# The recurrent branch of the second mixer in one stage: seven doubling levels inside 128-token tiles in place of 16-token chunks

## The chip, the cores and the metric

The kernel runs on one core of a Trainium2 chip. The metric is the device time of one execution in microseconds (us). A core has five engines that run their own instruction streams and meet at semaphores: PE (matmul; its weight loads are a row of their own, PEld, and overlap it), DVE (vector), ACT (scalar, with function tables that have to be loaded), POOL (GpSimd) and SP, which here issues the DMAs. SBUF and PSUM have 128 partitions; a tile "128x512" has 512 numbers in each.

## The reference

Two transformer blocks run one after the other over 512 tokens of width 1024. The second block's mixer has two halves: an attention group (its result is `n_otok` in the kernel, 8 heads of 64) and a gated linear recurrence. Their outputs, 512 wide each, are laid side by side and multiplied by `w_out` (1024 by 1024). The recurrence, for each of 4 heads with 128 key and 128 value features:

```
qf = silu(q);  f = lb + (1 - lb) * sigmoid(z);  logf = log(max(f, 1e-30))
kf = (1 - lb) * sigmoid(-z);  vf = i_in
for chunks of 64 tokens:
    b = cumsum(logf)                                  # inside the chunk
    decay[t, s] = exp(b[t] - b[s])  for s <= t, else 0   # one per key feature
    a[t, s] = sum_d qf[t, d] * decay[t, s, d] * kf[s, d]
    o = a @ vf + (qf * exp(b)) @ state
    state = exp(b_last) * state + (kf * exp(b_last - b)).T @ vf
o = o * rsqrt(mean(o * o) + 1e-6) * out_norm;  o = o * silu(g_in)
```

The size of the chunk is free: any tiling that gives the same sums is the same function. All of it is float32.

## The kernel before

The program is a row of stages; each is a block in which the five engines run their own lists of instructions, and ends in a meeting of all of them, after which SP clears the stage's semaphores. Nothing of the next stage, its DMAs included, is issued before that. The order of the work on each engine is the order in which the Python code writes it; there is no scheduler.

`x_hi`/`x_lo` hold a float32 tensor as two parts in a faster format. A dense product is three matmuls (`three_products`, L51 to L56): high by high, high by low, low by high. Weights are split the same way while they stream in: ACT makes the high part, POOL or DVE subtracts it from the raw panel for the low part. A matmul of plain float32 operands shows in the trace as two MATMUL records.

Four stages stand between the last attention stage (`att2`) and the second feed-forward stage (`ffn2`):

1. `turn_to_features` (L1167): the attention result is transposed by 16 PE transposes and split into `x_hi[:, :4]`, `x_lo[:, :4]`.
2. `hgrn_operands` (L2187): loads the 16 projected panels (4 MB, each of the four groups `z`, `inp`, `q`, `gate` 1 MB), and makes sigmoids, logarithms, a scan that sums the logs inside chunks of 16 tokens, and exponentials of the sums; transposes values and keys to token-major (`h_vtok`, `h_wtok`).
3. `hgrn_outputs` (L2336): works on chunks of 16 tokens. Inside a chunk, each distance `j` from 0 to 15 between query and key is a round: DVE subtracts the shifted log sums (L2531), ACT takes the exponential (L2488), POOL multiplies by the keys (L2520), DVE multiplies by the queries (L2567) and sums over features (L2570) into `ho_weights`. Beside it, 31 state steps go from chunk to chunk: PE makes the chunk's update `ho_kv` (L2427, 4 matmuls), DVE adds it to the decayed state (L2550, 4 instructions), PE reads the state with the chunk's queries (L2435, 4 matmuls of 16 columns). 27 of the steps are written between the rounds on DVE (`steps_by`, `BESIDE`), 4 behind them. Then 16 DMAs place the weights in a DRAM scratch, one DMA loads them back as full 128x128 matrices (`ho_inner`), PE multiplies them with the values (L2455), and the result is normed (a ones-matmul, four 128x512 reciprocals at L2584) and gated. The attention half of the output projection, 8 panels (`out_panel`, L54 to L56 with tile `ho_bank`), is written on PE behind all the state steps: four panels before L2455, four beside the norm.
4. `project_onto` (L763, tiles `wo_`): the recurrence's half of the output projection, 8 panels of 12 matmuls, added to `hT` by DVE (L385).

Of the kernel before, what the change touches and what calls it, by code (L numbers as in the profile page):

```python
# [13 lines left out]
P = 128  # L14
# [2119 lines left out]
def second_mixer(nc, hT, x_hi, x_lo, d):  # L2134
    with ExitStack() as ctx:
# [48 lines left out]
N_PROJ3 = 16  # L2184


def hgrn_operands(nc, projections, proj, ident, write, fold, ends, v_tok, w_tok, lower_bound):  # L2187

    with ExitStack() as ctx:
        c = Chip(nc, ctx)
        lb = c.sb("hf_lb", [P, HG_HEADS])
        lb_e = c.sb("hf_lbe", [P, HG_HEADS])
        free = c.sb("hf_free", [P, HG_HEADS])
        sig = c.sb("hf_sig", [P, HG_HEADS, SEQ])
        tiny = c.sb("hf_tiny", [P, HG_HEADS, SEQ])
        inside = c.sb("hf_inside", [P, HG_HEADS * SEQ])  # L2200
        part = c.sb("hf_part", [P, 1], I32)
        odd = c.sb("hf_odd", [P, 1], I32)
        parity = c.sb("hf_parity", [P, 2])
        banks = [c.ps(f"hf_bank{i}", [P, SEQ]) for i in range(4)]
        S = {x: c.sem(f"hf_{x}") for x in ("lb", "lb_shift", "lb_exp", "const", "sigmoids", "f", "seq", "logs",
                                           "b", "eb", "rest", "erest", "w", "turned", "taken")}
        landed = {x: c.sem(f"hf_landed{x}") for x in (HQ, HF, HI, HG)}
        q, z, inp, gate = (proj[:, x:x + 4, :] for x in (HQ, HF, HI, HG))

# [3 lines left out]
        def chunked(x):  # L2213
            return flat(x).rearrange("p (c i) -> p c i", i=CHUNK)
        HALF = [slice(0, 2), slice(2, 4)]
        PART = 2.0 ** -50
        with nc.Block() as block:
            @block.sync
            def _(sp):
                sp.dma_start(lb[:], lower_bound).then_inc(S["lb"], 16)  # L2220
                for x in (HF, HI, HQ, HG):
                    sp.dma_start(proj[:, x:x + 4, :], projections[x:x + 4].rearrange("n p s -> p n s")
                                 ).then_inc(landed[x], 16)

            @block.gpsimd
            def _(pool):
                pool.memset(inside[:], 1.0).then_inc(S["const"], 1)
                pool.iota(part[:], pattern=[[0, 1]], base=0, channel_multiplier=1).then_inc(S["const"], 1)
                pool.wait_ge(S["const"], 2)
                pool.memset(inside[:].rearrange("p (c i) -> p c i", i=CHUNK)[:, :, 0:1], 0.0  # L2230
                            ).then_inc(S["const"], 1)

            @block.scalar
            def _(act):
                act.wait_ge(S["lb_shift"], 1)
                act.activation(lb_e[:], lb_e[:], ACT.Exp).then_inc(S["lb_exp"], 1)
                act.wait_ge(landed[HF], 16)
                for e in HALF:
                    act.activation(flat(sig[:, e]), flat(z[:, e]), ACT.Sigmoid).then_inc(S["sigmoids"], 1)
                for e in HALF:  # L2240
                    act.activation(flat(write[:, e]), flat(z[:, e]), ACT.Sigmoid, scale=-1.0
                                   ).then_inc(S["sigmoids"], 1)
                act.wait_ge(landed[HQ], 16)
                act.activation(flat(q), flat(q), ACT.Silu).then_inc(S["sigmoids"], 1)
                act.wait_ge(landed[HG], 16)
                act.activation(flat(gate), flat(gate), ACT.Silu).then_inc(S["sigmoids"], 1)
                for n, e in enumerate(HALF):
                    act.wait_ge(S["f"], 2 * n + 2)
                    act.activation(flat(z[:, e]), flat(z[:, e]), ACT.Ln).then_inc(S["logs"], 1)
                    act.activation(flat(tiny[:, e]), flat(tiny[:, e]), ACT.Ln, scale=1.0 / PART  # L2250
                                   ).then_inc(S["logs"], 1)
                for n, e in enumerate(HALF):
                    act.wait_ge(S["b"], n + 1)
                    act.activation(flat(tiny[:, e]), flat(z[:, e]), ACT.Exp).then_inc(S["eb"], 1)
                    act.wait_ge(S["rest"], n + 1)
                    act.activation(flat(sig[:, e]), flat(sig[:, e]), ACT.Exp).then_inc(S["erest"], 1)

            @block.vector
            def _(dve):
                done = [0]  # L2260

                def then(instruction):
# [4 lines left out]
                dve.wait_ge(S["const"], 3)  # L2267
                then(dve.tensor_scalar(odd[:], part[:], CHUNK.bit_length() - 1, 1, ALU.logical_shift_right,
                                       ALU.bitwise_and))
                then(dve.tensor_copy(parity[:, 1:2], odd[:]))  # L2270
                then(dve.tensor_scalar(parity[:, 0:1], parity[:, 1:2], -1.0, 1.0, ALU.mult, ALU.add))

                dve.wait_ge(S["lb"], 16)
                dve.tensor_tensor(lb_e[:], lb[:], lb[:], ALU.subtract).then_inc(S["lb_shift"], 1)
# [5 lines left out]
                for n, e in enumerate(HALF):  # L2280
# [497 lines left out]
```

## Time and profile before

| | us |
|---|---|
| median of three runs | 3402.12 (3399.36 to 3403.47) |
| the profiled execution | 3402.71 |
| its span | 3401.0 |
| from the first transpose of stage 1 to the first DMA of `ffn2` | 2731.79 to 2999.65 |

| engine | busy us | share of the span | instructions |
|---|---|---|---|
| PE | 3071.7 | 90% | 14558 |
| PEld | 2598.3 | 76% | 14558 |
| DVE | 1909.9 | 56% | 3857 |
| ACT | 1061.0 | 31% | 1477 |
| POOL | 869.4 | 26% | 509 |

The shares are means over the whole program. The change touches one stretch of 268 us near its end, so that stretch is what has to be read. PEclk in the rows is the granted clock of TensorE as a share of 2.4 GHz: 1.00 is 2.4 GHz and 0.50 is 1.2 GHz.

### The profile page before, as it was taken

Reading aid. Unit: us, or ns where it says so; the run is one execution under the profiler, and the core shown is the slowest. Engines: PE = TensorE matmul, PEld = TensorE weight load, DVE = VectorE, ACT = ScalarE, POOL = GpSimd, SP = SyncE. Lnnn points to the kernel's source line nnn. Section 1 sums busy time; section 2 is a strip of 40 time slices with the busy share of each in tenths; the row PEclk is TensorE's granted clock in tenths of the full one; section 3 lists DMA queues with packets and bytes.
Section 4 is the critical chain, followed back from the end, with each engine's and each line's share of the span. In section 5 each row is a group of like instructions: output and inputs, shape, how many; then the busy total and the mean of one; then the engine's idle time right before and its main releaser. Section 6 shows DMA issues by size and latency. Waiting matters only on the chain. (4 is left out here: it accounts for less than half of the span.)

```text
span 3401.0 us, 41723 instructions
## 1 busy us (share of the span) xinstructions
PE 3071.7 (90%) x14558; PEld 2598.3 (76%) x14558; DVE 1909.9 (56%) x3857; ACT 1061.0 (31%) x1477; POOL 869.4 (26%) x509
## 2 busy tenths in 40 slices
PE   7669879999899999899999989998869958789997
PEld 6447667888688888699999978887657748668885
DVE  5565444866577770188888754434225468554433
ACT  3222331333244443233333333223113341132321
POOL 0013200444333334486666300000412123100000
PEclk9769989999999999899999999999869965799998
DMA  4013232344345555499999823332212020123331
GB/s 136 18 43 106 99 105 81 127 137 133 120 143 185 183 177 175 154 368 378 353 356 352 294 82 98 99 99 87 113 41 75 32 79 0 40 92 99 93 99 62
DMA packets 183698, 469.15 MB, mean 138 GB/s; under 512 B 23937, under 2 KB 75777, under 8 KB 181890
## 3 DMA queue, kind: packets, MB, share of 16 engines
q1 hardware_dynamic: 159874, 374.93, 33.4%
q0 software_dynamic: 22528, 67.19, 5.2%
q10 hardware_dynamic: 1152, 25.17, 1.8%
q8 instruction: 83, 1.36, 0.2%
q14 instruction: 61, 0.50, 0.0%
HBM read 396.49 MB, written 70.52 MB: 137 GB/s over the span
## 5 line engine op out<-in xcount | busy, mean ns | idle before, releaser
L54 PE MATMUL cb_y<-cb_g_hi,cb_b_hi 128*128 128x384 f32 x1024 | 343.1, 335 | 15.0 <-DVE cb_g_lo L1746 15.0
L55 PE MATMUL cb_y<-cb_g_lo,cb_b_hi 128*128 128x384 f32 x1024 | 342.9, 335 | 0.0
L56 PE MATMUL cb_y<-cb_g_hi,cb_b_lo 128*128 128x384 f32 x1024 | 342.8, 335 | 0.0
L186 DVE TENSOR_TENSOR ffn_lo<-ffn_raw,ffn_hi 128x1024 fp32r<-128x1024 f32 x132 | 161.4, 1225 | 271.1 <-ACT ffn_hi L182 271.1
L54 PE MATMUL ffn_bank<-x_hi,ffn_hi 128*128 128x512 f32 x704 | 277.5, 394 | 23.0 <-DVE x_lo L122 20.2
L55 PE MATMUL ffn_bank<-x_lo,ffn_hi 128*128 128x512 f32 x704 | 275.4, 391 | 0.0
L56 PE MATMUL ffn_bank<-x_hi,ffn_lo 128*128 128x512 f32 x704 | 275.1, 391 | 0.0
L491 POOL TENSOR_TENSOR bs_lo<-bs_raw,bs_hi 128x1024 fp32r<-128x1024 f32 x72 | 174.7, 2427 | 320.3 <-ACT bs_hi L468 320.3
L54 PE MATMUL bs_ps<-x_hi,bs_hi 128*128 128x512 f32 x576 | 232.3, 403 | 14.8 <-POOL bs_lo L491 14.8
L182 ACT CAST ffn_hi<-ffn_raw 128x1024 fp32r<-128x1024 f32 x132 | 137.9, 1048 | 298.9 <-PE ffn_bank L56 260.0
L56 PE MATMUL bs_ps<-x_hi,bs_lo 128*128 128x512 f32 x576 | 226.8, 394 | 0.0
L1722 ACT CAST cb_b_hi<-cb_b_raw 128x1024 fp32r<-128x1024 f32 x128 | 134.6, 1052 | 294.6 <-PE cb_y L56 267.1
L55 PE MATMUL bs_ps<-x_lo,bs_hi 128*128 128x512 f32 x576 | 225.1, 391 | 0.0
L54 PEld LDWEIGHTS cb_y<-cb_g_hi,cb_b_hi 128*128 128x128 f32 x1024 | 192.9, 188 | 15.4 <-DVE cb_b_lo L1743 15.4
L1806 POOL DMA_INDIRECT cb_rows<-in_peer_v,ex_chosen x128 | 186.9, 1460 | 59.8 <-issue 36.7
L1743 DVE TENSOR_TENSOR cb_b_lo<-cb_b_raw,cb_b_hi 128x1024 fp32r<-128x1024 f32 x128 | 156.6, 1224 | 79.9 <-ACT cb_b_hi L1722 79.9
L1603 DVE TENSOR_SCALAR br_col<-ex_iota,br_slot 128x128 f32<-128x128 f32 x384 | 196.0, 510 | 0.0
L491 POOL TENSOR_TENSOR rs_lo<-rs_raw,rs_hi 128x1024 fp32r<-128x1024 f32 x56 | 149.8, 2677 | 179.6 <-ACT rs_hi L468 179.6
L55 PEld LDWEIGHTS cb_y<-cb_g_lo,cb_b_hi 128*128 128x128 f32 x1024 | 192.9, 188 | 0.0
L56 PEld LDWEIGHTS cb_y<-cb_g_hi,cb_b_lo 128*128 128x128 f32 x1024 | 192.8, 188 | 0.0
L1787 POOL DMA_INDIRECT cb_units_of<-hidden,ex_chosen x128 | 152.6, 1193 | 116.9 <-DVE cb_total L1752 79.6
L54 PE MATMUL rs_ps<-x_hi,rs_hi 128*128 128x512 f32 x448 | 177.6, 396 | 0.5 <-POOL rs_lo L491 0.5
(483 smaller groups left out, 6992.0 us busy)
## 6 DMA issues: line engine op xcount, KB each, us to landing
cb_b_raw<-in_peer_v SPq DMA_DIRECT2D x128, 512.0 KB, 7.0
ffn_raw<-in_gu SPq DMA_DIRECT2D x88, 512.0 KB, 3.5
bs_raw<-in_peer_u SPq DMA_DIRECT2D x72, 512.0 KB, 3.6
rs_raw<-in_peer_u SPq DMA_DIRECT2D x56, 512.0 KB, 3.6
routing<-br_out ACTq DMA_DIRECT2D x8, 3072.0 KB, 9.1
cb_route<-routing SPq DMA_DIRECT2D x32, 768.0 KB, 9.2
cb_unit<-hidden SPq DMA_DIRECT2D x128, 192.0 KB
ffn_raw<-in_down SPq DMA_DIRECT2D x44, 512.0 KB, 3.5
```

What stands on the lines that cost most here:

```text
L54: pe.matmul(out, w_high, x_high, start=first, stop=False)
L55: pe.matmul(out, w_high, x_low, start=False, stop=False)
L56: return pe.matmul(out, w_low, x_high, start=False, stop=last)
L182: act.copy(hi[:, k % R, :], raw[:, k % R, :]).then_inc(high, 1)
L186: dve.tensor_tensor(lo[:, k % R, :], raw[:, k % R, :], hi[:, k % R, :].bitcast(F32), ALU.subtract).then_inc(split, 1)
L491: eng.tensor_tensor(self.lo[:, s, :], self.raw[:, s, :], self.hi[:, s, :].bitcast(F32), ALU.subtract).then_inc(self.split, 1)
L1603: last = dve.tensor_scalar(col_hot[:, k, b, :], iota[:], slot[:, k, 1, b:b + 1], None, ALU.is_equal)
L1722: act.copy(b_hi[:, j, :], b_raw[:, j, :]).then_inc(b_high, 1)
L1743: dve.tensor_tensor(b_lo[:, j, :], b_raw[:, j, :], b_hi[:, j, :].bitcast(F32), ALU.subtract).then_inc(b_split, 1)
L1787: pool.indirect_dma_start(units_of[:, n:n + 1], None, flat, bass.IndirectOffsetOnAxis(chosen[:, 1, n:n + 1], 0)).then_inc(units_landed[n / ...
L1806: pool.indirect_dma_start(rows[:, n % V, :], None, table, bass.IndirectOffsetOnAxis(chosen[:, 0, n:n + 1], 0)).then_inc(rows_landed[n % V] ...
```

## The change

The four stages become one, `hgrn_stage`. Inside a 128-token tile the scores are made in seven levels of doubling. At level `n` (block size 2^n) a query in the second half of a pair of blocks meets the keys in the first half: `qp` holds the query times the decay from its block's start, `kr` the key times the decay to its block's end, so their product is one matmul per head and tile, of which only the blocks next to each other are wanted. A mask, made by POOL, picks these out of PSUM into `hg_pairs` by `copy_predicated`. Then DVE doubles the blocks: late queries are multiplied by the total of the early block, early keys by the total of the late one. Logarithms, scan and exponentials fall away (the decays are products of `f`). The state goes from tile to tile in three steps in place of 31. The 16 (head, tile) pairs are cut in two halves `e` of 8, so that PE and DVE can take turns. The output projection is one loop over 16 half-width panels with a ring of four buffers; panels 0 to 7 (attention half) are written between the levels. The norm squares token-major results with an accumulating ACT instruction, so the reciprocal is 128x4 and no ones-matmul is left. `hg_scratch` and its 18 DMAs are gone.

```diff
-        hgrn(nc, hT, x_hi, x_lo, o_tok, ident, d)
-
-    project_onto(nc, "wo2", x_hi[:, 4:8, :], x_lo[:, 4:8, :], d["w_out"][:, :, 4 * P:], hT)
+        hgrn_stage(nc, d["hg_proj"], o_tok, ident, d["lower_bound"], d["out_norm"], d["w_out"], x_hi, x_lo, hT)
...
+                def load_out(k):
+                    if k >= R:
+                        sp.wait_ge(S["split"], k - R + 1)
...
+                sp.dma_start(lb[:], lower_bound).then_inc(S["lb"], 16)
+                load(HF)
+                load_out(0)
+                load_out(1)
+                load(HQ)
+                load(HI)
+                load_out(2)
+                load_out(3)
+                load(HG)
...
+                def level(n, e):
+                    if n:
+                        pe.wait_ge(S["doubled"], 2 * (n - 1) + e + 1)
+                        pe.wait_ge(S["masked"], 2 * (n - 1) + e + 1)
+                    else:
+                        pe.wait_ge(S["key"], e + 1)
+                        pe.wait_ge(S["query"], e + 1)
+                    for i in range(HT):
+                        a = e * HT + i
+                        to = s_ps[e][:, i * P // 2:(i + 1) * P // 2].rearrange("p (b i) -> p b i", i=1 << n)
+                        last = pe.matmul(to, flat(kr[:])[:, a * P:(a + 1) * P], second_half(flat(qp[:]), 1 << n, a),
+                                         start=True, stop=True)
+                    last.then_inc(S["scored"], 1)
...
+                pe.wait_ge(S["o_low"], 4)
+                out_panel(0)
+                out_panel(1)
+                level(0, 0)
+                level(0, 1)
...
+                same_token(0)
+                same_token(1)
+                for n in range(1, LEVELS):
+                    level(n, 0)
+                    level(n, 1)
+                    if n < 5:
+                        out_panel(n + 1)
+                pe.wait_ge(S["doubled"], 2 * LEVELS)
+                pe.wait_ge(S["masked"], 2 * LEVELS)
+                turn_keys(0)
+                turn_keys(1)
...
+                write(0)
+                pe.wait_ge(S["state"], 1)
+                turn_keys(2)
+                out_panel(6)
+                write(1)
+                read(1)
+                write(2)
+                out_panel(7)
+                turn_result(0)
+                read(2)
+                read(3)
+                for t in range(1, TILES):
+                    turn_result(t)
+                pe.wait_ge(S["y_low"], TILES)
+                for k in range(n_out // 2, n_out):
+                    out_panel(k)
...
+                def double(n, e):
+                    dve.wait_ge(S["scored"], 2 * n + e + 1)
...
+                    dve.tensor_tensor(late, late, both[:, :, 0:1].broadcast_to(late.shape), ALU.mult)
+                    dve.tensor_tensor(early, early, both[:, :, 1:2].broadcast_to(early.shape), ALU.mult)
+                    dve.tensor_tensor(totals[n + 1][:, e * half // 2:(e + 1) * half // 2], both[:, :, 0], both[:, :, 1],
+                                      ALU.mult).then_inc(S["doubled"], 1)
...
+                def place(n, e):
...
+                    dve.copy_predicated(to[:, :, :, 1, :], mask.broadcast_to(shape),
+                                        s_ps[e][:].rearrange("p (a b i) -> p a b i", a=HT, i=size)
+                                        ).then_inc(S["masked"], 1)
...
+                for n in range(LEVELS):
+                    for e in range(2):
+                        if n == 0:
+                            dve.wait_ge(S["paired"], e + 1)
+                        double(n, e)
+                        place(n, e)
+                    if n == 1:
+                        place_same(0)
+                        place_same(1)
+                    if 2 <= n <= 5:
+                        add_out(n)
```

DVE before, in the 16 rounds of stage 3; `ho_pair` is the work tile of a round, `ho_state` the state:

```order
L2531 TENSOR_TENSOR ho_pair<-ho_b 128x1536
L2550 SCALAR_TENSOR_TENSOR ho_state<-ho_state,h_ends,ho_kv 128x128 x8
L2567 TENSOR_TENSOR ho_pair<-ho_pair,ho_q 128x1792
L2570 TENSOR_REDUCE ho_weights<-ho_pair 128x14
L2531 TENSOR_TENSOR ho_pair<-ho_b 128x1408
L2550 SCALAR_TENSOR_TENSOR ho_state<-ho_state,h_ends,ho_kv 128x128 x12
L2567 TENSOR_TENSOR ho_pair<-ho_pair,ho_q 128x1664
```

DVE now, at level 2 and the first half of level 3; `hg_qp` and `hg_kr` are the folded queries and keys, `hg_total` the block totals, `hg_s` the PSUM tile of scores:

```order
L2486 TENSOR_TENSOR hg_qp<-hg_qp,hg_total 128x128x4
L2487 TENSOR_TENSOR hg_kr<-hg_kr,hg_total 128x128x4
L2488 TENSOR_TENSOR hg_total<-hg_total 128x128
L2501 COPY_PREDICATED hg_pairs<-hg_masks,hg_s 128x128x4
L2486 TENSOR_TENSOR hg_qp<-hg_qp,hg_total 128x128x4
L2487 TENSOR_TENSOR hg_kr<-hg_kr,hg_total 128x128x4
L2488 TENSOR_TENSOR hg_total<-hg_total 128x128
L2501 COPY_PREDICATED hg_pairs<-hg_masks,hg_s 128x128x4
L2474 TENSOR_TENSOR hT<-hT,hg_out 128x512
L2486 TENSOR_TENSOR hg_qp<-hg_qp,hg_total 128x64x8
```

A round of three instructions over up to 2048 numbers and 8 to 12 small state instructions has become a level half of four instructions over at most 512, with the addition of one output panel behind each level.

PE before, in the same place (`ho_kv` the update of the state, `ho_o` the read):

```order
L2427 MATMUL ho_kv<-h_vtok,h_wtok 128x128 x4
L2435 MATMUL ho_o<-h_fold,ho_state 128x16 x4
L2427 MATMUL ho_kv<-h_vtok,h_wtok 128x128 x4
L2435 MATMUL ho_o<-h_fold,ho_state 128x16 x4
L2427 MATMUL ho_kv<-h_vtok,h_wtok 128x128 x4
```

PE now, at levels 4 to 6 and just behind them (a panel is 12 rows of L54 to L56, the last two of panel 5 are shown; `hg_ktok` and `hg_vtok` are keys and values by token):

```order
L55 MATMUL hg_out<-x_lo,hg_hi 128x512
L56 MATMUL hg_out<-x_hi,hg_lo 128x512
L2306 MATMUL hg_s<-hg_qp,hg_kr 128x64 x32
L2322 MATMUL hg_s<-n_ident,hg_kr 128x128 x8
L2380 MATMUL hg_o<-hg_vtok,hg_pairs 128x128 x16
L2330 MATMUL hg_s<-hg_vtok,hg_ktok 128x128 x4
L2322 MATMUL hg_s<-n_ident,hg_kr 128x128 x4
L54 MATMUL hg_out<-x_hi,hg_hi 128x512
```

The dense panels, which stood behind the whole recurrence, now stand between the levels; levels 5 and 6 (the x32 row) have none beside them.

## Rows read from the trace of the kernel before

**Rows 1.** Windows: us, each engine's busy us (instructions), granted clock, DMA share, GB/s.
```profile
2737.70:2780.20 42.50, 7.35 (x32) 6.55 (x32) 30.26 (x44) 21.18 (x19) 2.21 (x3) 0.55 0.28 99
...
2790.00:2903.80 113.80, 99.78 (x425) 92.65 (x425) 97.34 (x151) 19.08 (x20) 46.57 (x18) 0.51 0.02 5
2903.80:2920.50 16.70, 16.70 (x72) 15.69 (x73) 4.49 (x16) 0.00 (x0) 0.00 (x0) 0.50 0.31 72
...
2934.50:2967.50 33.00, 19.36 (x89) 13.53 (x87) 28.03 (x25) 10.33 (x16) 3.87 (x3) 0.89 0.05 16
2967.50:2999.60 32.10, 23.54 (x96) 19.00 (x96) 10.61 (x17) 4.96 (x8) 0.00 (x0) 0.84 0.22 66
```

**Rows 2.** Timeline: start us, us, engine, line, op, tiles, count; edges of the four stages.
```profile
2731.79 3.59 PE L1180 MATMUL on_turn_bank<-n_ident,n_otok 128*128 128x128 f32 x16 [2.23 <-PEq L44]
...
2738.10 2.47 SPq L2222 DMA_DIRECT2D h_proj<-hg_proj  x4
...
2743.98 2.00 ACT L2239 ACTIVATE hf_sig<-h_proj 128x1024 f32<-128x1024 f32 x2 [1.71 <-DMA h_proj<-hg_proj]
...
2965.04 2.49 DVE L2594 TENSOR_TENSOR x_lo<-ho_q,x_hi 128x512 fp32r<-128x512 f32 x4
...
2970.39 10.19 SPq L336 DMA_DIRECT2D wo_raw<-in_w_out  x8
2999.65 0.33 SPq L77 DMA_DIRECT2D ffn_gain<-in_ffn_norm  x1
```

**Rows 3.** Groups by line, 2731 to 3000: busy us, mean ns, idle before, releaser.
```profile
L2427 PE MATMUL ho_kv<-h_vtok,h_wtok 32*128 32x128 f32 x248 | 62.1, 426 | 0.0
...
L2550 DVE SCALAR_TENSOR_TENSOR ho_state<-ho_state,h_ends,ho_kv 128x128 f32<-128x128 f32 x120 | 33.6, 342 | 23.7 <-PE ho_kv L2427 23.2
L2567 DVE TENSOR_TENSOR ho_pair<-ho_pair,ho_q 128x2048 f32<-128x2048 f32 (+15 forms) x16 | 31.4, 1960 | 1.2 <-POOL ho_pair L2520 1.2
```

**Rows 4.** Timeline of PE, plain float32 matmuls; one call is two records.
```profile
2679.86 1.00 PE L625 MATMUL att_o<-n_vsel,att_probsT 128*128 128x64 f32 x8
...
2852.41 2.07 PE L2427 MATMUL ho_kv<-h_vtok,h_wtok 32*128 32x128 f32 x8
...
2934.49 3.73 PE L2455 MATMUL ho_o<-ho_inner,h_vtok 128*128 128x128 f32 x32
```

**Rows 5.** Timeline of the 8 panels of `project_onto`: first matmul, last addition.
```profile
2974.42 0.79 PE L54 MATMUL wo_ps<-x_hi,wo_hi 128*128 128x512 f32 x1 [16.86 <-DVE wo_lo L370]
...
2998.00 0.69 DVE L385 TENSOR_TENSOR hT<-hT,wo_ps 128x512 f32<-128x512 f32 x1 [2.03 <-PE wo_ps L56]
```

**Rows 6.** Groups by line and shape: busy us, mean ns of one, idle before.
```profile
L255 DVE TENSOR_TENSOR ffn_prod<-ffn_scaled 128x512 f32<-128x512 f32 x44 | 30.5, 692 | 2.0 <-ACT ffn_scaled L224 0.7
...
L2584 DVE RECIPROCAL ho_b<-ho_q 128x512 f32<-128x512 f32 x4 | 13.4, 3341 | 0.0
...
L569 DVE TENSOR_SCALAR yb<-att_o,att_inverse 128x128 f32<-128x128 f32 x16 | 5.6, 351 | 2.6 <-PE att_o L625 2.1
...
L2291 DVE TENSOR_SCALAR n_otok<-n_otok,hf_free 128x512 f32<-128x512 f32 x4 | 1.9, 484 | 0.1
```

**Rows 7.** Same view, ACT and POOL.
```profile
L584 ACT ACTIVATION_READ_ACCUMULATOR att_probs<-att_biased,att_shift 128x1 f32 x80 | 14.9, 186 | 0.0
...
L2481 ACT CAST ho_out_hi<-ho_out_raw 128x512 fp32r<-128x512 f32 x8 | 4.9, 620 | 37.9 <-PE ho_bank L56 37.9
...
L2488 ACT ACTIVATE ho_pair<-ho_pair 128x128 f32<-128x128 f32 x1 | 0.3, 311 | 1.2 <-DVE ho_pair L2531 1.2
...
L2511 POOL TENSOR_TENSOR ho_out_lo<-ho_out_raw,ho_out_hi 128x512 fp32r<-128x512 f32 x8 | 11.6, 1449 | 51.3 <-ACT ho_out_hi L2481 51.3
```

**Rows 8.** Windows, columns as in rows 1: the granted clock in three stretches.
```profile
2640.00:2729.00 89.00, 89.00 (x467) 65.05 (x466) 37.78 (x158) 33.41 (x77) 11.61 (x5) 1.00 0.10 33
2850.00:2880.00 30.00, 28.55 (x121) 26.35 (x120) 25.74 (x45) 4.01 (x4) 9.37 (x4) 0.50 0.00 1
...
2959.00:2962.00 3.00, 0.00 (x0) 0.00 (x0) 3.00 (x3) 0.62 (x1) 0.00 (x0) 0.75 0.00 0
```

More of the change, by code:

```diff
@@ new lines, in hgrn_stage @@
+        kr = c.sb("hg_kr", [P, HG_HEADS, SEQ])
+        qp = c.sb("hg_qp", [P, HG_HEADS, SEQ])
+        totals = [f[:].rearrange("p h s -> p (h s)")] + [
+            c.sb(f"hg_total{n}", [P, HG_HEADS * SEQ >> n])[:] for n in range(1, LEVELS + 1)]
+        pairs = c.sb("hg_pairs", [P, HG_HEADS * TILES, P])
+        masks = c.sb("hg_masks", [P, LEVELS, P // 2])
+        v_tok = c.sb("hg_vtok", [P, TILES, HG_HEADS * P])
+        k_tok = c.sb("hg_ktok", [P, TILES - 1, HG_HEADS * P])
+        state = c.sb("hg_state", [P, TILES - 1, HG_HEADS, P])
@@ L2243, in _ @@
+                out_high(0)
+                out_high(1)
                 act.wait_ge(landed[HQ], 16)
-                act.activation(flat(q), flat(q), ACT.Silu).then_inc(S["sigmoids"], 1)
-                act.wait_ge(landed[HG], 16)
[L2246 to L2256, printed above, removed]
+                for e in HALF:
+                    act.activation(flat(q[:, e]), flat(q[:, e]), ACT.Silu).then_inc(S["silu"], 1)
+                for t in range(TILES):
+                    act.wait_ge(S["v_turned"], t + 1)
+                    act.copy(v_tok[:, t, :], o_ps[t][:]).then_inc(S["v_copied"], 1)
@@ new lines, in _ @@
+                out_high(2)
+                out_high(3)
+                act.wait_ge(landed[HG], 16)
+                act.activation(flat(gate), flat(gate), ACT.Silu).then_inc(S["gated"], 1)
+                for k in range(R, R + 6):
+                    out_high(k)
+                for t in range(TILES - 1):
+                    act.wait_ge(S["k_turned"], t + 1)
+                    act.copy(k_tok[:, t, :], s_ps[t % 2][:]).then_inc(S["k_copied"], 1)
+                square(0)
+                out_high(R + 6)
@@ new lines, in mean, with norm @@
+                def mean(t):
+                    dve.wait_ge(S["squared"], t + 1)
+                    dve.tensor_scalar(root[:, t], squares[:, t], 1.0 / P, EPS, ALU.mult, ALU.add).then_inc(S["mean"], 1)
+                def norm(t):
+                    dve.wait_ge(S["root"], t + 1)
+                    dve.reciprocal(inverse[:, t], root[:, t]).then_inc(S["inverse"], 1)
+                    dve.wait_ge(S["inverse"], t + 1)
+                    for h in range(HG_HEADS):
+                        cols = slice(h * P, (h + 1) * P)
+                        last = dve.tensor_scalar(y_tok[:, t, cols], o_ps[t][:, cols], inverse[:, t, h:h + 1], None, ALU.mult)
+                    last.then_inc(S["normed"], 1)
@@ new lines, in _ @@
+                norm(0)
+                add_out(6)
+                step(2)
+                add_out(7)
+                mean(1)
+                norm(1)
+                gated(0)
+                mean(2)
+                norm(2)
+                low_result(0)
+                gated(1)
+                mean(3)
+                norm(3)
+                low_result(1)
+                gated(2)
+                low_result(2)
+                gated(3)
+                low_result(3)
+                for k in range(n_out // 2, n_out):
+                    add_out(k)
@@ L2615, in final_norm @@
+    clear_semaphores(nc, [*S.values(), *landed.values(), *out_landed])
 def final_norm(nc, hT, gain, out):
```

560 lines of the change are left out of this document (230 added, 330 removed).

## The prediction, written before the changed kernel had run

> **What bounds the kernel now.** I read the shares of the engines first: PE is busy for 90% of the span, which says that time comes only from stretches in which PE does little dense work. The windows then show the stretch of the change, 2731.7 to 2999.6, and what each engine does in it [rows 1]. Its longest piece is the 113.8 us of the 16 rounds, 2790.0 to 2903.8. There DVE is busy for 97.3 us and PE for 99.8, yet PE does no dense product: its clock stands at 0.51, and its work is 128-column updates and 16-column reads. The groups by line say what DVE's 97 us are: 33.6 us are 120 state instructions of 0.342 us, and 31.4 us one of the three instructions of a round [rows 3]. State steps and rounds share DVE, so both are the bound; a step waits for PE too (23.2 us under L2550). Behind the loop come 16.7 us of last steps, while the weights go through DRAM; 33.0 us in which DVE is busy for 28.0, with four reciprocals of 3.34 us [rows 1, 6]; and 32.1 us for `project_onto`, 7 of them before its first matmul [rows 1, 2, 5]. In front, `hgrn_operands` takes 42.5 us with PE busy for 7.4. From the first transpose at 2731.8 to the first DMA of `ffn2` at 2999.7 it is 267.9 us [rows 2]. `ffn2` starts from nothing, so all that the stretch loses, the kernel loses.
>
> **The change, step by step.** I lay the new stage out from T, its first transpose. A hand-off is left out of each step and comes as one term at the end.
>
> *To panels 0 and 1: T+20.0.* The 16 transposes take 3.6 us [rows 2]. The first projection load (1 MB) lands 5.9 us after its issue (2738.1 to 2744.0), so at about T+6.1; before, it was issued only after stage 1. Then ACT has four sigmoids of 1.0 us each (2.00 for two, rows 2), so the high parts of panels 0 and 1 (0.62 each, rows 7), written behind them, end at 11.3, and POOL's low part, 1.45 as a mean [rows 7], at 12.6 with what DVE makes it slower. POOL's two memsets and 14 mask instructions have until T+10.6, more than 0.6 us each, and are hidden. PE has idled since T+3.6 and starts low: eight panels from a standstill take 24.3 us with the last addition, 2974.4 to 2998.7 [rows 5]; with 2.8 us for a panel at 2.4 GHz (12 matmuls of 0.234), the first costs some 4.6. Two panels: 7.4, to T+20.0. DVE's keys and queries are ready at T+16, beside it.
>
> *Level 0, values, same-token scores: T+33.0.* A level half is 8 matmuls of 64 columns. The nearest row is L625: four calls of that size in 1.00 us at 2.4 GHz, so 2.0 per half [rows 4]. Bounds: 1.9 by the 128-column L2455 (16 calls in 3.73, so 0.23 each), 4.1 by L2427 at 1.2 GHz (0.52 each). Both halves 4.0, to 24.0; value transposes 1.8; 16 same-token calls of 128 columns 3.7, to 29.6. DVE may not fold before the same-token scores are taken. Its half of level 0 is three multiplications and one masked copy over 512 numbers. Multiplications are 0.692 [rows 6], 0.62 start to start. `copy_predicated` is in no row; by the nearest (a two-operand 128x512) it is 0.69, below it 0.48 (L2291, one operand), above it 3.34 (L2584, the slowest of this size). I take 0.69. The second half ends at 33.0.
>
> *Levels 1 to 4: T+58.2.* PE does half, half, panel: 2.0 + 2.0 + 2.8 = 6.8. DVE does two halves of 2.2 to 2.4 and one addition of 0.69: at most 5.4 (level 1 has four masked copies more, 7.8, once). So PE is the bound, and DVE's work lies under the panel. Level 1 starts at 30.4 and waits for DVE's second half: its panel ends at 37.8. Three more periods make 58.2. Panels 2 to 5 cost nothing of their own here; before, all eight attention panels stood behind the steps.
>
> *Levels 5 and 6: T+69.4.* No panel is left, so the engines take turns: PE half 2.0, DVE half 2.2, with the other half between, plus an addition. 11.2.
>
> *Values and state: T+84.8.* Transposes 0.9, 16 matmuls of `hg_pairs` with the values 3.7, first write 0.9, DVE's copy 0.7, transposes 0.5, panel 6 2.8, write, read, write 2.8 (0.93 each, rows 4), panel 7 2.8. The chain of 31 steps, 3.8 us apart where PE sets it (2.07 for the update, the rest the read), is now three.
>
> *Norm: T+102.7.* ACT squares a tile in four pieces of 0.31 + 0.19, 2.0 us [rows 7]; DVE norms it with four of 0.351 [rows 6], about 1.3 with the small reciprocal; gate and low part 0.7 each, high part 0.62. ACT and DVE wait on each other tile by tile: behind panel 7, 3.2 us until the first tile is gated, then 5.7 for each of the next two, and 3.3 for the last gate, high and low part: 17.9. The four reciprocals (13.4 us) go.
>
> *Panels 8 to 15: T+127.0.* They wait for the last low part, PE has idled: 24.3 as in rows 5.
>
> *What I add.* 4 us for hand-offs that no neighbour hides (some 40 at 0.1; my bounds are 0 and 10), and the clearing of 50 semaphores. `hgrn_outputs` cleared 32 between 2967.5 and 2970.4, 2.9 us [rows 2]; I take 3.4.
>
> Sum: 127.0 + 4 + 3.4 = 134.4 in place of 267.9, so 133.5 saved. The profiled execution has 3402.7 (span 3401.0, 1.7 around it), which is 0.6 above the median of the runs. 3402.7 - 133.5 = **3269 us**.
>
> **Whether the clock holds.** PE was fully busy in the attention stage at 1.00, with 64-column matmuls between dense ones, and busy for 28.55 of 30 us in the rounds at 0.50 [rows 8]. So being busy did not bring the clock up. The levels look like the first of these as long as panels are between them, and I count 2.4 GHz; in levels 5 and 6 the waits are under 3 us, and the clock fell in a wait of about that length [rows 8]. The Trainium skill ("TensorE: Matmul & The Clock Gate", "Part 1: The HAM clock gate") says that the gate opens by how busy the PE has been; by it the levels would run at 2.4 GHz and the sum stands. The 28.55 of 30 us at 0.50 speak against taking it at its word, and so the next case has a chance.
>
> **The rivals.**
>
> *A: the clock stays at 1.2 GHz through the levels.* For: the rounds' 0.50. Against: the attention stage's 1.00. A half costs 4.1, a panel 5.1, a period 13.3: +26 for levels 1 to 4, +11 for level 0 with transposes and same-token scores, +10 for levels 5 and 6, +8 for values and state. 3269 + 55 = 3324. If it falls only in levels 5 and 6 and behind, +15: 3284.
>
> *B: DVE is dearer than I count,* by masked copies or by the short runs of 1 to 64 numbers that the levels read. 18 masked copies at 3.34 would be +48 on DVE. PE's slack in levels 1 to 4 (1.4 each) hides 6: 3269 + 42 = 3311. At twice 0.69, which two passes over the data would be, +12 less 6: 3275. Then DVE sets the period of the levels.
>
> *C: slower than before.* Every fold and masked copy works on patterns of short runs and repeated elements, and PE and DVE wait on each other at each of the 14 halves, so a price per run has no cover. There are 46 instructions of 512 numbers (28 folds, 14 + 4 masked copies) and two full-size totals. To eat 133.5 us plus 6 of slack they need 2.9 us more each, 3.6 in all, above the slowest row of that size, 3.34 [rows 6]. At 4.0 us each: 3269 + 48 * 3.3 - 6 = 3421.
>
> *D: the stage gives back what it gains elsewhere.* `ffn2` loads and normalizes only after it, so nothing speaks for this.
>
> **How the numbers follow.** The forecast, with DVE and PE near the nearest rows, has 0.62 and by itself 3255 to 3285: hand-offs of 0 to 10 us, a partly low clock, masked copies up to twice 0.69. A has 0.15 (3284 to 3324), B beyond double 0.18 (3275 to 3311), C 0.02, D 0.01, and 0.02 are left for a stage shorter than 3255. The range for 8 in 10 leaves out the ends of A, B and C: 3250 to 3308. About 0.2% is what a measurement of this kernel can tell from no change; A and B are both far below 3395, so faster 0.97, within 0.2% 0.01, slower 0.02.
>
> **What would show it right or wrong.** The new stage spans 134 us. The level matmuls stand 0.25 us apart under a granted clock near 1.00, periods of levels 1 to 4 are 6.8 us with PE without a wait, and `hg_qp`, `hg_kr` and `hg_pairs` rows read 0.69. Levels 5 and 6 take 11 us, the norm 18, and the last eight panels 24. A shows as 0.50 in the levels' windows; B as masked copies or folds over 1 us and PE waiting for DVE in levels 1 to 4; C as DVE rows over 3.6. I am wrong in the mechanism if the stage is 134 us but PE waits in loaded levels, or if the saving is not in the rounds and steps.

## The result and the profile after

The changed kernel takes **3269.84 us** (median of 4 runs, 3269.61 to 3272.06) beside 3401.69 for the kernel before (4 runs, 3399.36 to 3403.47): a ratio of 0.9614, 95% interval 0.9598 to 0.9631. The forecast was 3269 us. The profiled execution took 3270.03, its span is 3268.0.

The new stage starts with its first transpose at T = 2732.37, and `ffn2` issues its first DMA at 2867.44: 135.1 us, where the forecast had 134.4 and the kernel before 267.9 [rows 2]. From that DMA to the end of the span it is 400.6 us after and 401.3 before, so the saving lies in the stage. The windows show the stage piece by piece, with the columns of [rows 1].

```profile
2732.40:2744.40 12.00, 3.64 (x17) 3.27 (x17) 8.17 (x17) 9.79 (x13) 9.55 (x18) 0.50 0.84 307
2744.40:2751.90 7.50, 7.50 (x24) 6.03 (x25) 5.16 (x6) 2.16 (x3) 1.52 (x1) 0.72 0.77 279
2751.90:2761.00 9.10, 9.10 (x81) 8.84 (x79) 2.19 (x3) 4.92 (x8) 2.27 (x2) 1.00 0.01 2
2761.00:2765.30 4.30, 0.08 (x2) 0.06 (x1) 4.30 (x4) 1.00 (x2) 4.04 (x3) 1.00 0.60 170
2765.30:2776.50 11.20, 11.20 (x45) 10.21 (x46) 10.10 (x15) 0.00 (x0) 0.00 (x0) 0.54 0.10 29
2776.50:2795.50 19.00, 19.00 (x134) 17.50 (x133) 14.70 (x29) 1.86 (x3) 3.80 (x3) 1.00 0.14 42
2795.50:2806.00 10.50, 7.55 (x66) 7.31 (x65) 8.64 (x18) 0.62 (x1) 1.27 (x1) 1.00 0.07 27
2806.00:2822.60 16.60, 15.81 (x101) 14.58 (x102) 4.83 (x16) 5.95 (x22) 1.28 (x1) 0.90 0.06 17
2822.60:2838.80 16.20, 4.80 (x33) 3.73 (x31) 10.25 (x27) 5.69 (x24) 0.15 (x1) 0.74 0.00 0
2838.80:2864.10 25.30, 24.53 (x96) 19.74 (x96) 5.50 (x8) 2.49 (x4) 6.29 (x5) 0.89 0.03 10
```

What was 130.5 us of rounds and last steps before, 2790.0 to 2920.5 [rows 1], is now the 54.1 us of levels with their panels (2751.9 to 2806.0) and part of the 16.6 us behind them. The 132.8 us that the stage saves lie in three places: 38.6 ahead of the rounds (58.2 us from the first transpose to 2790.0 before, 19.6 to the first level now), 76.4 in the rounds and last steps (130.5, now 54.1), and 17.7 behind them (79.1, now 61.4). In levels 2 to 4 PE is busy for all of 19.00 us at a clock of 1.00. The timeline of the same stage (start us, us, engine, line, operation, tiles, count, the wait before it) holds the edges, and the one place that went otherwise than forecast.

```profile
2751.93 3.68 PE L2306 MATMUL hg_s<-hg_qp,hg_kr 128*128 128x64 f32 x32
2755.44 1.92 PE L2364 MATMUL hg_o<-n_ident,hg_all 128*128 128x128 f32 x16
2757.21 3.84 PE L2316 MATMUL hg_o<-hg_all,hg_kr 128*128 128x128 f32 x32
2758.73 6.31 POOL L2280 TENSOR_TENSOR hg_lo<-hg_raw,hg_hi 128x512 fp32r<-128x512 f32 x4 [12.81 <-ACT hg_hi L2408]
2759.50 1.07 DVE L2486 TENSOR_TENSOR hg_qp<-hg_qp,hg_f 128x512 f32<-128x512 f32 x1 [6.68 <-PE hg_o L2316]
2760.48 1.76 DVE L2487 TENSOR_TENSOR hg_kr<-hg_kr,hg_f 128x512 f32<-128x512 f32 x1
2762.17 1.74 DVE L2488 TENSOR_TENSOR hg_total<-hg_f 128x512 f32<-128x512 f32 x1
2763.83 1.29 DVE L2501 COPY_PREDICATED hg_pairs<-hg_masks,hg_s 128x512 f32<-128x512 uint32 x1
...
2765.27 6.68 PE L2306 MATMUL hg_s<-hg_qp,hg_kr 128*128 128x64 f32 x32 [4.22 <-DVE hg_pairs L2501]
2771.71 0.77 PE L54 MATMUL hg_out<-x_hi,hg_hi 128*128 128x512 f32 x1
...
2776.49 3.68 PE L2306 MATMUL hg_s<-hg_qp,hg_kr 128*128 128x64 f32 x32
...
2779.99 0.70 DVE L2501 COPY_PREDICATED hg_pairs<-hg_masks,hg_s 128x512 f32<-128x512 uint32 x1
...
2782.83 3.68 PE L2306 MATMUL hg_s<-hg_qp,hg_kr 128*128 128x64 f32 x32
...
2805.96 1.30 PE L2322 MATMUL hg_s<-n_ident,hg_kr 128*128 128x128 f32 x8 [2.40 <-DVE hg_pairs L2501]
...
2838.84 0.79 PE L54 MATMUL hg_out<-x_hi,hg_hi 128*128 128x512 f32 x1 [3.56 <-DVE x_lo L2551]
...
2867.44 0.33 SPq L77 DMA_DIRECT2D ffn_gain<-in_ffn_norm  x1
```

A level is one row of 32 records in 3.68 us, 1.75 per half. The next level starts 6.3 us later, and PE does not wait. Level 1 is the exception: DVE starts level 0 at 2759.50, when the same-token scores of the first half are taken; its first three multiplications take 1.07, 1.76 and 1.74 us where most later ones of that size take 0.69, the masked copy takes 1.29, and PE stands still for 4.22 us. The clock is still 1.00 in that wait and falls to 1.2 GHz as PE comes back (0.54 in the window, 6.68 us for the same 32 records, 0.77 for the first matmul of panel 2), and level 1 with its panel takes 11.2 us where the later levels take 6.3.

### The profile page after: what moved, and what is told of

Its sections match the earlier page's. It is cut to its first block and busy times, and to the rows that moved or that the text cites. A ratio compares the mean times of both kernels' runs of the same rounds, so it can differ in the third digit from the quotient of the medians.

```text
span 3268.0 us, 41012 instructions
## 1 busy us (share of the span) xinstructions
PE 2983.4 (91%) x14322; PEld 2521.2 (77%) x14322; DVE 1804.2 (55%) x3734; ACT 1029.6 (32%) x1475; POOL 844.8 (26%) x511
## 5 line engine op out<-in xcount | busy, mean ns | idle before, releaser
L54 PE MATMUL cb_y<-cb_g_hi,cb_b_hi 128*128 128x384 f32 x1024 | 343.2, 335 | 15.0 <-DVE cb_b_lo L1743 15.0
L56 PE MATMUL cb_y<-cb_g_hi,cb_b_lo 128*128 128x384 f32 x1024 | 342.8, 335 | 0.0
L54 PE MATMUL ffn_bank<-x_hi,ffn_hi 128*128 128x512 f32 x704 | 277.7, 394 | 25.2 <-DVE x_lo L122 23.1
L56 PE MATMUL ffn_bank<-x_hi,ffn_lo 128*128 128x512 f32 x704 | 275.4, 391 | 0.0
L54 PE MATMUL bs_ps<-x_hi,bs_hi 128*128 128x512 f32 x576 | 232.3, 403 | 14.8 <-POOL bs_lo L491 14.8
L56 PE MATMUL bs_ps<-x_hi,bs_lo 128*128 128x512 f32 x576 | 226.9, 394 | 0.0
L54 PEld LDWEIGHTS cb_y<-cb_g_hi,cb_b_hi 128*128 128x128 f32 x1024 | 192.9, 188 | 15.5 <-DVE cb_b_lo L1743 15.4
L56 PEld LDWEIGHTS cb_y<-cb_g_hi,cb_b_lo 128*128 128x128 f32 x1024 | 192.9, 188 | 0.0
L54 PE MATMUL rs_ps<-x_hi,rs_hi 128*128 128x512 f32 x448 | 177.6, 396 | 0.5 <-POOL rs_lo L491 0.5
```

What stands on the lines that cost most here:

```text
L54: pe.matmul(out, w_high, x_high, start=first, stop=False)
L56: return pe.matmul(out, w_low, x_high, start=False, stop=last)
```

## The experiments

The theory at this point: the stage is as forecast, and the 6 us at level 1 come from three things in a row: POOL's subtractions slow DVE down, masked copies with short runs cost twice as much, and PE's wait lets the clock fall. The rivals are given with each run. Times are medians; kernels of one group share their runs of the kernel before: 3400.41 (8 runs) for the first four, 3401.32 (9 runs) for the last four. The time from the stage's first transpose to `ffn2`'s first DMA in the profiled execution is given beside them: ahead of the stage all these kernels are the same, and yet that transpose starts between 2728.1 (run 7) and 2732.8 (run 1), so some us of a difference between two executions can lie outside the stage.

### 1 and 2. Rounds and steps of the kernel before, each alone

*Steps only* takes the 16 rounds out of the kernel before, on DVE, ACT and POOL:

```diff
-                for j in range(CHUNK):
-                    x = pair[:, j % 3, :CHUNK - j, :]
-                    if j + 2 < CHUNK:
-                        diff(j + 2)
...
-                for n in range(BESIDE, N_CHUNKS - 1):
+                for n in range(N_CHUNKS - 1):
                     step(n)
```

> The kernel before without the 16 rounds: the scores inside a chunk are left out, the 31 state steps stay. Theory (PE's chain of updates and reads at 1.2 GHz bounds the loop as much as DVE's rounds): 31 steps of about 3.8 us are 118 us, so the stretch from the first update (2790) to the last read (2920.5) shrinks by only 10 to 15 us, and the kernel reads 3385 to 3395. Rival (the rounds are the bound, the steps lie in their shade and would run in about half the time alone): the loop falls to 60 to 75 us and the kernel to 3340 to 3355.

*Rounds only* takes the 31 steps out, on PE and DVE:

```diff
-                for n in range(N_CHUNKS):
-                    if n < N_CHUNKS - 1:
...
-                            last = pe.matmul(kv_ps[n % 2][:, h, :], w_tok[rows, n % 2, tile, cols],
...
-                for n in range(BESIDE, N_CHUNKS - 1):
-                    step(n)
```

> The kernel before without the 31 state steps: the state and its part of the output are left out, the 16 rounds stay. Theory (rounds and steps share DVE): DVE's three instructions of a round are 74 us in all, with the start and the turns between engines some 80 to 85 in place of 113.8, and the 16.7 us of last steps go as far as the DMAs of the weights do not need them. Panels 0 to 3 come before the loop's end. Kernel 3402 - 30 - 25 = 3347, 3335 to 3360. Rival (POOL and ACT bound the rounds): the rounds stay near 100 us and the kernel near 3370.

Measured: steps only 3384.14 (ratio 0.9952, 0.9936 to 0.9968), rounds only 3350.06 (0.9851, 0.9832 to 0.9871). So taking the rounds away alone saves 16 us, a little more than expected, and the steps alone 50, as expected; the stretch to `ffn2` has 251.4 and 216.7 us in place of 267.9. First a window of *steps only*, then the first matmul behind the rounds in *rounds only*.

```profile
2850.00:2920.00 70.00, 70.00 (x299) 63.57 (x298) 18.47 (x60) 3.52 (x6) 5.15 (x4) 0.58 0.04 12
```

```profile
2867.45 0.77 PE L54 MATMUL ho_bank<-x_hi,ho_out_hi 128*128 128x512 f32 x1 [66.99 <-DVE hT L2518]
```

Without rounds PE is busy for 70.00 of 70.00 us, with the steps and from 2903.89 with the panels: the steps are a chain of their own on PE, and DVE is nearly free (18.47). From the first update (2790.75) to panel 0 (2903.89) the steps take 113.1 us alone, of 130.5 with the rounds. Without steps PE stands still for 66.99 us while DVE, ACT and POOL do the rounds, and the first DMA of the weights is issued at 2866.80 instead of 2903.85. The two lay beside each other, and each hid most of the other. That is why a change to these two saves more than 50 us only if it takes both away. No run takes both away and leaves the rest of the four stages as it was, and none separates what made the 38.6 us ahead of the rounds.

### 3. What a masked copy costs, and what POOL does to DVE

The changed kernel with a row of DVE instructions behind the stage, each of 128x512 numbers and each waiting for the one before; at the end the same beside POOL's subtractions. They write only buffers that are no longer read.

```diff
+                    masked(0, 0, s_ps[0][:])
+                    masked(1, 1, s_ps[0][:])
+                    masked(2, 2, s_ps[0][:])
+                    masked(6, 6, s_ps[0][:])
+                    masked(6, 0, s_ps[0][:])
+                    masked(0, 6, s_ps[0][:])
+                    masked(0, 0, from_sbuf)
+                    masked(2, 2, from_sbuf)
+                    plain(0, s_ps[0][:])
+                    plain(2, s_ps[0][:])
+                    fold(0)
```

> The changed kernel with a row of DVE instructions of 512 numbers behind its stage, first with POOL idle, then with POOL subtracting. Theory P (the pattern written): a masked copy into runs of 1 or 2 numbers takes 1.29 us, into runs of 4 or more 0.70, whatever the mask and the source; an ordinary multiplication into the same runs takes 0.69. Rival M (the mask's contents or its repeats): with the mask of level 0 in the layout of level 6 it takes 1.29 as well. Rival S (PSUM as source): from SBUF the masked copy of level 0 takes 0.70. Under POOL's subtractions (two SBUF operands) theory C (DVE and POOL share the way to SBUF) says that multiplications with two SBUF operands go from 0.69 to 1.1 to 1.8, and those with one PSUM operand stay at 0.7.

The first number is the level whose pattern is written (runs of 2 to that power), the second the mask. The kernel took 3305.89 us in its one run, 36 of it for the added row. Its timeline:

```profile
2863.93 1.29 DVE L2643 COPY_PREDICATED hg_pairs<-hg_masks,hg_s 128x512 f32<-128x512 uint32 x1 [0.32 <-PEq L2238]
2865.25 1.29 DVE L2643 COPY_PREDICATED hg_pairs<-hg_masks,hg_s 128x512 f32<-128x512 uint32 x1
2866.58 0.69 DVE L2643 COPY_PREDICATED hg_pairs<-hg_masks,hg_s 128x512 f32<-128x512 uint32 x1
...
2868.06 0.72 DVE L2643 COPY_PREDICATED hg_pairs<-hg_masks,hg_s 128x512 f32<-128x512 uint32 x1
2868.82 1.29 DVE L2643 COPY_PREDICATED hg_pairs<-hg_masks,hg_s 128x512 f32<-128x512 uint32 x1
2870.14 1.30 DVE L2643 COPY_PREDICATED hg_pairs<-hg_masks,hg_all 128x512 f32<-128x512 uint32 x1
...
2872.21 0.69 DVE L2650 TENSOR_TENSOR hg_pairs<-hg_s,hg_masks 128x512 f32<-128x512 f32 x1
...
2884.94 14.67 POOL L2626 TENSOR_TENSOR hg_lo<-hg_raw,hg_hi 128x512 fp32r<-128x512 f32 x10 [30.85 <-DVEq L2670]
2884.95 2.93 DVE L2643 COPY_PREDICATED hg_pairs<-hg_masks,hg_s 128x512 f32<-128x512 uint32 x4
2887.91 6.55 DVE L2656 TENSOR_TENSOR hg_qp<-hg_qp,hg_f 128x512 f32<-128x512 f32 x4
2894.50 2.87 DVE L2650 TENSOR_TENSOR hg_pairs<-hg_s,hg_masks 128x512 f32<-128x512 f32 x4
```

The price follows the pattern that is written: 1.29 us for runs of one and of two numbers, 0.69 for runs of four, 0.72 in the pattern of level 6 even with level 0's mask (2868.06), 1.29 the other way round (2868.82), and the same from SBUF (`hg_all`, 2870.14). A multiplication into level 0's pattern takes 0.69. So only masked copies pay, and only at levels 0 and 1: theory P, not the mask (M) or the source (S). The second question has as clear an answer: beside POOL, a multiplication with both operands in SBUF goes from 0.69 to 1.6 us (6.55 for four), while a masked copy or a multiplication that reads scores from PSUM stays at 0.7, as theory C has it. That is what slowed level 0 in the changed kernel, where POOL made the low parts of panels 2 to 5 at that moment. The Trainium skill ("GPSIMD Engine Reference", section "1. Specifications") says that GpSimd's SBUF interfaces are shared with VectorE, with contention for VectorE instructions with two SBUF inputs; by these rows the trace agrees, 1.6 against 0.7 us.

### 4. The low parts of panels 2 to 5 earlier

ACT's high parts, and with them POOL's low parts, move ahead of the value copies, so POOL is done before DVE starts level 0:

```diff
+                out_high(2)
+                out_high(3)
+                out_high(4)
+                out_high(5)
...
-                out_high(2)
-                out_high(3)
...
-                for k in range(R, R + 6):
+                for k in range(R + 2, R + 6):
```

> The changed kernel with the high parts of panels 2 to 5 made on ACT before the value copies instead of behind them, so that POOL's low parts are not beside DVE's first level half. Theory (that half was slowed by POOL from 3.1 to 5.5 us, PE waited 4.2 us for it and came back at 1.2 GHz): the half takes 3.1 to 3.6 us, PE waits under 2 us, level 1 and panel 2 run at 2.4 GHz, and the stage loses 5 to 7 us: kernel 3263 to 3265. Rival (the half is slow by its patterns of single numbers): nothing moves, 3269 to 3270. If the clock falls all the same, only 2 to 3 us go: 3267.

Measured: 3265.26 us (3263.91 to 3268.45; ratio 0.9603, 0.9587 to 0.9619), 4.6 less than the changed kernel; the stage has 131.9 us instead of 135.1, so 3.2 of it lie there. One line of DVE's timeline, then PE's, then two windows:

```profile
2758.54 0.70 DVE L2488 TENSOR_TENSOR hg_qp<-hg_qp,hg_f 128x512 f32<-128x512 f32 x1 [6.68 <-PE hg_o L2316]
...
2761.78 1.97 PE L2306 MATMUL hg_s<-hg_qp,hg_kr 128*128 128x64 f32 x16 [1.69 <-DVE hg_pairs L2503]
2764.70 3.60 PE L2306 MATMUL hg_s<-hg_qp,hg_kr 128*128 128x64 f32 x16 [0.95 <-DVE hg_pairs L2503]
2768.05 0.77 PE L54 MATMUL hg_out<-x_hi,hg_hi 128*128 128x512 f32 x1
```

```profile
2762.00:2766.00 4.00, 3.05 (x23) 2.94 (x22) 4.00 (x8) 0.00 (x0) 0.00 (x0) 0.84 0.00 0
2766.00:2772.00 6.00, 6.00 (x21) 5.18 (x21) 4.88 (x8) 0.00 (x0) 0.00 (x0) 0.53 0.00 0
```

The multiplications are back at 0.70 and the wait of 4.22 is now two of 1.69 and 0.95: about 2.5 us of the first wait were POOL's, the rest is DVE's own half behind the same-token scores. The clock falls all the same, in the second half of level 1 (3.60 us instead of 1.97), so the theory is right on DVE and wrong on the clock, and the gain in the stage is nearer to the 2 to 3 us of that case.

### 5. The panels behind the levels

This asks what the panels between the levels do: fill PE's time, or hold its clock as well.

```diff
                 for n in range(1, LEVELS):
                     level(n, 0)
                     level(n, 1)
-                    if n < 5:
-                        out_panel(n + 1)
...
                 write(0)
+                for k in range(2, 6):
+                    out_panel(k)
```

DVE's four additions move behind the levels with them, and ACT makes its first two key copies ahead of the high parts of panels 6 to 9, which can't start before the panels have run.

> The changed kernel with the four panels 2 to 5 of the norm taken from between the levels and put behind level 6. Theory (the levels pass from TensorE to VectorE and back, and the panels only fill TensorE while VectorE works): some 11 us of panel work stand alone behind the levels, and the four levels 1 to 4 take about 4.4 us each in place of 6.3 to 6.8, so the time is 3 to 5 us above the changed kernel, 3273 to 3275 us, with the granted clock at 1.00 in the levels. Rival (the panels also keep TensorE's clock at 2.4 GHz): without them the windows of the levels show 0.5 to 0.7, each level takes 6 us or more all the same, and the time is 3280 to 3290 us.

Measured: 3283.37 us (3279.74 to 3285.07; 0.9653, 0.9638 to 0.9668), 13.5 above the changed kernel; the stage has 148.6 us, 13.5 more as well. My theory (3273 to 3275) is wrong, the rival (3280 to 3290) right. The windows of level 1 and 2, of levels 3 to 6, and of the products with the values behind them:

```profile
2761.50:2775.20 13.70, 13.65 (x64) 13.49 (x64) 12.45 (x20) 0.00 (x0) 0.00 (x0) 0.51 0.07 21
2775.70:2803.30 27.60, 27.54 (x128) 27.38 (x128) 16.02 (x32) 0.00 (x0) 0.00 (x0) 0.50 0.00 1
...
2805.40:2811.90 6.50, 6.45 (x40) 6.48 (x41) 0.00 (x0) 1.17 (x2) 0.00 (x0) 0.68 0.01 3
```

PE comes to level 1 after the same wait of 4.22 us, and the clock never comes back in the levels: PE is busy for 41.2 of 41.3 us with 64-column matmuls at 1.2 GHz, 6.9 us per level, where a level with a panel takes 6.3 at 2.4 GHz. It rises in the 16 products of 128 columns behind them. In the changed kernel it rose in panel 2, and then stayed at 1.00 over levels 2 to 6. So the panels bring the clock back. Whether they also hold it is not shown: in this run it was at 0.51 before there was anything to hold, and levels 5 and 6 of the changed kernel keep 1.00 for 10.5 us without a panel. The Trainium skill ("TensorE: Matmul & The Clock Gate", "What's actually happening") says that the gate goes by how busy the PE has been. In the second of these windows PE is busy for 27.54 of 27.60 us by the profile and stays at 0.50, as in the rounds of the kernel before [rows 8]; by the profile's account of busy the trace does not agree.

### 6. Another order in the norm

In `hgrn_norm`'s piece PE is busy for 4.8 of 16.2 us. ACT made the squares of tiles 2 and 3 only after the high parts of tiles 0 and 1, which wait for DVE's gates. Now the squares come first, and on DVE, not shown here, the gates of tiles 1 and 2 stand ahead of the low part of tile 0:

```diff
-                high_result(0)
...
-                high_result(1)
...
-                high_result(2)
-                high_result(3)
+                for t in range(TILES):
+                    high_result(t)
```

> The changed kernel with the orders of ScalarE and VectorE in the norm behind the levels rearranged: the squares of tiles 1 to 3 stand ahead of the high parts, and VectorE's gate and low parts follow in tile order. Theory (this piece is a chain of ScalarE and VectorE with TensorE waiting, 4.8 us busy of 16.2): 3 to 5 us less, 3265 to 3267 us. Rival (VectorE alone bounds the piece, its order does not matter): 3269 to 3271 us.

Measured: 3260.26 us (3259.92 to 3263.53; 0.9583, 0.9568 to 0.9598), 9.6 less than the changed kernel, where I expected 3 to 5. Its window of that piece:

```profile
2821.90:2833.10 11.20, 4.46 (x33) 3.45 (x31) 9.96 (x27) 5.57 (x24) 0.14 (x1) 0.85 0.00 0
```

The piece goes from 16.2 to 11.2 us, DVE busy for 9.96 of it: the chain of two engines has become DVE's own time. The stage is 129.1 us instead of 135.1, so the profile shows 6.0 of the 9.6, a little more than the theory had; the profiled execution was the slowest of its four (3263.53), and what the other three had less is not in any trace.

### 7 and 8. The panels forward, and all together

*Panels forward* takes run 4 and puts panel 2 ahead of level 1, so that it fills PE's wait, panels 3 to 7 between levels 1 to 5, and none among the state steps.

```diff
+                out_panel(2)
                 for n in range(1, LEVELS):
...
-                    if n < 5:
-                        out_panel(n + 1)
+                    if n < 6:
+                        out_panel(n + 2)
...
-                out_panel(6)
...
-                out_panel(7)
```

> The changed kernel with the high parts ahead of the value copies, panel 2 of the norm ahead of level 1 and panels 3 to 7 between levels 1 to 5. Theory (TensorE's idle time ahead of level 1 lets the clock fall): the wait ahead of level 1 is under 0.5 us, the granted clock stays at 1.00 through level 1, level 1 takes 6.3 us as levels 2 to 4 do, and the time is 7 to 10 us below the changed kernel, 3259 to 3262 us. Rival (what is gained there is given back where panels 6 and 7 covered the value phase): 3264 to 3267 us.

Measured: 3260.35 us (3259.15 to 3261.50; 0.9585, 0.9570 to 0.9599), 9.5 less than the changed kernel, as the theory had it. The stage has 128.5 us, which is 6.6 less than the changed kernel's and 3.4 less than run 4's. Level 1 in its timeline, then the window of level 1 and its panel:

```profile
2759.70 1.89 PE L2306 MATMUL hg_s<-hg_qp,hg_kr 128*128 128x64 f32 x16
2761.79 1.97 PE L2306 MATMUL hg_s<-hg_qp,hg_kr 128*128 128x64 f32 x16 [0.19 <-DVE hg_pairs L2502]
```

```profile
2759.50:2763.50 4.00, 3.81 (x34) 3.66 (x32) 4.00 (x7) 0.62 (x1) 1.28 (x1) 1.00 0.13 27
2763.50:2770.50 7.00, 6.62 (x48) 6.04 (x47) 7.00 (x11) 0.62 (x1) 1.28 (x1) 1.00 0.16 53
```

The wait is 0.19 us, the clock stays at 1.00, and level 1 with its panel takes 6.7 us (2759.70 to 2766.38) in place of 11.2. Some was given back: from the first key transposes behind level 6 to panel 8 it is 29.5 us, beside 32.9 in the changed kernel with 5.6 us of panels in it, so 2.2 us more without them.

*All together* adds the orders of run 6 to run 7 (its diff is those two).

> The changed kernel with the rearranged norm orders, the high parts ahead of the value copies and the panels moved forward, all three together. If they add up: 3255 us (3253 to 3258). If the value phase gives back what level 1 gains: 3260 to 3264 us.

Measured: **3255.05 us** (5 runs, 3253.34 to 3257.47), 0.9567 of the kernel before (0.9554 to 0.9581), and 14.8 less than the changed kernel: faster than both, and within what was expected if they add up. Its stage takes 122.1 us, 13.0 less, where runs 6 and 7 took off 6.0 and 6.6. Level 1 in its windows:

```profile
2761.00:2770.50 9.50, 9.33 (x58) 8.21 (x58) 9.49 (x14) 0.62 (x1) 1.27 (x1) 1.00 0.08 28
```

## Why the prediction was right, step by step

The total was right to 1 us, but that it is so close is luck: the steps add up to it with errors of both signs (us from T, or the length of the piece):

| piece | forecast | measured |
|---|---|---|
| panels 0 and 1 done | T+20.0 | T+19.6 |
| same-token scores done on PE | T+29.6 | T+28.7 |
| level 1's panel done | T+37.8 | T+44.1 |
| levels 2 to 4, each | 6.8 | 6.3 |
| levels 5 and 6 | 11.2 | 10.5 |
| values and state | 15.4 | 16.6 |
| norm | 17.9 | 16.2 |
| panels 8 to 15 | 24.3 | 25.3 |
| hand-offs | 4.0 | in the pieces |
| clearing 50 semaphores | 3.4 | 3.3 |
| the stage | 134.4 | 135.1 |

- **That rounds and steps are both the bound** was the reading of [rows 1, 3]. Runs 1 and 2 show that neither alone is: 16 and 50 us alone, where the change takes 76.4 out of that stretch. The reason given, that they share DVE, holds for the rounds, which are 37 us shorter without the steps. The steps need no share of it to be slow: in run 1 they are PE's own chain at 1.2 GHz.
- **Where the saving lies.** By the prediction's own sign it had to be in the rounds and steps. Most of it is, 76.4 of 132.8 us, but 38.6 come from ahead of them, as the layout's T+20.0 for panels 0 and 1 implied. That these come from loads issued beside the transposes and from the logarithms, scan and exponentials that are gone is argued from the two orders of work; no run tests it.
- **The price of a level half.** Taken 2.0 from L625's 64-column calls, measured 1.75 (3.51 us from the first record of level 0 to the next group, for two halves). That is under the lower bound of 1.9 as well, since that came from 128-column calls.
- **Levels 1 to 4 hidden under PE.** True for 2 to 4, without a wait on PE. The step that failed is level 1: its panel ends 6.3 us late although the same-token scores were 0.9 early. Between the two the forecast has 8.2 us, waits of 0.8 and 0.6 and a period of 6.8; measured are 15.4, a wait of 4.22 and 11.2. It failed at DVE in level 0. Two of its prices were too low: the multiplication, where I took 0.69 from a row with no POOL work beside it and it was 1.07 to 1.76 (run 3 shows why), and the masked copy, 0.69 against 1.29 at two levels. At levels 2 to 6 the 0.69 holds, but for the first multiplication of levels 2 to 5 (0.83). I had used "up to twice 0.69" as rival B for all 18 masked copies; it holds for the four of levels 0 and 1, and "DVE sets the period of the levels" is seen nowhere behind level 1.
- **The clock.** "The levels look like the attention stage as long as panels are between them" held from level 2 on, and run 5 shows that the clock did not come back without them. Rival A came true in level 1, where PE came back from a wait; the low clock there costs 4.9 us (11.2 less 6.3 for the period). In levels 5 and 6, where I feared it, the clock was 1.00 through a wait of 0.55 us and one of 2.40 behind them. It fell as PE came back from the second, in the products with the values:

```profile
2806.00:2812.00 6.00, 6.00 (x40) 6.00 (x41) 0.00 (x0) 1.17 (x2) 0.00 (x0) 0.72 0.00 0
```

- **Values and state.** The 16 products with the values took 5.17 us in place of 3.7, which is more than the 1.2 us that the piece was over. The terms of the forecast for it add up to 15.1, not to the 15.4 of its line.
- **The norm** was 1.7 us shorter: ACT's four squares take 1.1 us, not the 2.0 that I had from adding 0.31 and 0.19. The next square starts 0.26 us after the one before, while the record of reading the sum still runs, as ACT's timeline has it:

```profile
2826.39 0.27 ACT L2413 ACTIVATE hg_all<-hg_o 128x128 f32<-128x128 f32 x1
2826.56 0.19 ACT L2413 ACTIVATION_READ_ACCUMULATOR hg_all<-hg_o 128x1 f32 x1
2826.65 0.27 ACT L2413 ACTIVATE hg_all<-hg_o 128x128 f32<-128x128 f32 x1
```

- **Hand-offs.** The 4 us were an estimate that covered, by luck, the net error of the other pieces, level 1 above all: they end at T+131.7 instead of T+127.0. As a size they are not shown.
- Rivals C and D are out: no fold took over 1.76 us, and `ffn2` is as long as before.

What stays open: which part of the 9.6 us of run 6 is real beyond the 6.0 in its profile; what made the 38.6 us ahead of the rounds; and after which waits the clock falls. It fell when PE took up its work after 4.22 us, after 1.69 and 0.95 (run 4), after 0.55 and 2.40 with level 6 between them, and after 2.29 (run 7, 5.36 us for the products with the values); it did not after 0.55 or 0.79 alone in the changed kernel, or after 0.19 in run 7. No run varies one wait alone.

## What to carry to other kernels

Before a chain is replaced because it fills the profile, find what runs beside it: two chains that hid each other gave 16 and 50 us alone, and the stretch that held them gave 76 when both went. Work that fills an engine's wait may also bring its clock back: without the four panels the levels ran at half the clock and took no less time than with them, and the panels' 11 us came on top; and the better place for filler was ahead of the first wait, not behind it (run 7). A price taken from a row is a price beside what ran there: look at what POOL does under a DVE instruction with two SBUF operands before using its 0.69.

## What the runs showed of the hardware

- A masked copy of 128x512 float32 (run 3 and the changed kernel's levels) takes 0.69 to 0.72 us when it writes runs of four or more numbers and 1.29 for runs of one or two, whatever the mask, and from PSUM as from SBUF. A multiplication into the same pattern takes 0.69.
- A float32 multiplication with two operands in SBUF goes from 0.69 to 1.6 us while POOL subtracts, with one operand in PSUM it stays at 0.7. POOL's own subtraction takes 1.59 us beside such multiplications, and 1.27 beside the others (run 3, its single records).
- TensorE stayed at 1.2 GHz through 41.2 us of 64-column float32 matmuls in run 5, broken by one wait of 0.55 us, and at 2.4 GHz through 64-column and 128-column ones (9.10 us, 2751.9 to 2761.0) where 512-column panels had gone before. It rose during panel 2 in the changed kernel (0.63 us a matmul, then 0.39).
